# Expert stages of a two-layer trunk: which rows the indirect DMAs move, the order of splitting, and 8 KB pieces of weights

## What is computed

```python
D_MODEL, N_EXPERTS, N_GROUPS, TOPK_EXPERTS, D_EXPERT = 1024, 16, 4, 2, 512

def grouped_moe(h, w_router, b_router, w_gate, w_up, w_down):
    probs = softmax(h @ w_router + b_router)
    g_sel = argmax over the 4 groups of the sum of the group's two best probs
    vals, idx = top_k(where(in group g_sel, probs, -inf), 2)
    gates = one_hot(idx) * (vals / sum(vals)), summed over the two
    y = 0
    for e in range(N_EXPERTS):
        a = silu(h @ w_gate[e]) * (h @ w_up[e])      # (tokens, 512)
        y = y + gates[..., e:e+1] * (a @ w_down[e])  # (tokens, 1024)
    return y
```

## Time and profile before

| | |
|---|---|
| Runs | 2278.16, 2268.29, 2274.32 us; median 2274.32 |
| Profiled execution | 2277.34 us, a span of 2275.6 |
| TensorE busy | 1903.2 us of the span (84%) |
| VectorE, ScalarE, GpSimd busy | 1089.5, 768.7, 239.6 us |
| Expert stage, layer 0 | 295.0 us (958.7 to 1253.7), TensorE busy 287.0, 363 GB/s |
| Expert stage, layer 1 | 294.4 us (1923.5 to 2217.9), TensorE busy 287.1, 359 GB/s |
| Weights read in a pair | 12 units of 1.049 MB |

### The profile page before, as it was taken

How to read it: one execution, slowest core, us unless ns; L and a number is a source line. 1 busy time by engine, 2 the same in 40 slices (tenths; PEclk the granted TensorE clock), 3 DMA queues, 4 the chain that set the end, 5 groups by cost and what they waited for, 6 DMA issues and landing times.

```text
span 2275.6 us, 20410 instructions
## 1 busy us (share of the span) xinstructions
PE 1903.2 (84%) x6689; PEld 1039.8 (46%) x6689; DVE 1089.5 (48%) x1674; ACT 768.7 (34%) x993; POOL 239.6 (11%) x235
## 2 busy tenths in 40 slices
PE   2899899999899997399999479996568972999990
PEld 0443323343233334187878134343343441877870
DVE  0320352210342017298988371126742173989886
ACT  0110211111211001388786211124442021888861
POOL 0000000000000000432221120000000003122201
PEclk8899999999999997699999789995775975999995
DMA  9232172423163124699998922021002233999983
GB/s 340 102 133 77 72 277 75 158 75 111 67 247 105 54 74 147 244 359 392 392 393 332 378 77 79 20 58 38 1 1 74 85 140 102 367 393 392 393 301 122
DMA packets 194993, 412.19 MB, mean 181 GB/s; under 512 B 14382, under 2 KB 18558, under 8 KB 194877
## 3 DMA queue, kind: packets, MB, share of 16 engines
q1 hardware_dynamic: 168962, 322.26, 39.5%
q0 software_dynamic: 21248, 72.02, 8.4%
q10 hardware_dynamic: 4712, 17.02, 2.1%
HBM read 363.36 MB, written 47.90 MB: 181 GB/s over the span
## 4 chain that ended last, share of the span: by engine, by line
PE 68%; DVE 11%; DMA 8%; issue 4%; DVEq 4%; ACT 3%; POOL 1%; POOLq 0%; ACTq 0%; SPq 0%
PE bank L586 34%; PE bank L884 17%; PE bank L579 3%; DMA RING<-in_w_mod 3%; PE bank L811 3%; DMA RING<-in_w_gate 3%; ACT WH L1319 2%; PE bank L796 2%; PE bank L977 1%; PE bank L785 1%; DVEq L2228 1%; PE bank L664 1%; POOL slot_d L1644 1%; DVE WL L2083 1%; PE bank L781 1%
## 5 line engine op out<-in xcount | busy, mean ns | idle before, releaser
L586 PE MATMUL bank<-RING,HT 128*128 128x512 f32 (+3 forms) x1600 | 685.8, 584 | 15.9 <-ACT HT L1146 13.3
L2083 DVE TENSOR_TENSOR WL<-RING,WH 128x2048 fp32r<-128x2048 f32 x192 | 436.7, 2293 | 81.1 <-ACT WH L1319 79.4
L586 PEld LDWEIGHTS bank<-RING,HT 128*128 128x128 f32 (+1 forms) x1600 | 263.8, 172 | 397.8 <-issue 377.5
L1319 ACT ACTIVATE WH<-RING 128x2048 fp32r<-128x2048 f32 x192 | 364.9, 1915 | 115.4 <-PE bank L884 92.4
L579 PE MATMUL bank<-cst,M 128*128 128x128 f32 (+3 forms) x721 | 114.2, 289 | 119.4 <-DMA M<-h_d,slot_c 71.8
L884 PE MATMUL bank<-WH,HGH 128*128 128x512 f32 x512 | 204.1, 399 | 3.0 <-DVE HGL L2094 3.0
L884 PE MATMUL bank<-WL,HGH 128*128 128x512 f32 x512 | 201.3, 393 | 0.0
L884 PE MATMUL bank<-WH,HGL 128*128 128x512 f32 x512 | 201.3, 393 | 0.0
L579 PEld LDWEIGHTS bank<-cst,M 128*128 128x128 f32 (+3 forms) x721 | 92.0, 156 | 178.3 <-DMA M<-h_d,slot_c 72.8
L586 PE MATMUL bank<-RING,M 128*128 128x512 f32 (+1 forms) x320 | 138.6, 593 | 0.3 <-ACT M L1268 0.3
L884 PE MATMUL bank<-WH,ATH 128*128 128x512 f32 x256 | 102.8, 402 | 14.4 <-DVE ATL L2110 14.4
(11 more groups left out here) (277 smaller groups left out, 2095.1 us busy)
## 6 DMA issues: line engine op xcount, KB each, us to landing
RING<-in_w_gate SPq DMA_DIRECT2D x64, 1024.0 KB, 12.1
RING<-in_w_up SPq DMA_DIRECT2D x64, 1024.0 KB
RING<-in_w_down SPq DMA_DIRECT2D x64, 1024.0 KB, 12.0
RING<-in_w_mod SPq DMA_DIRECT2D x24, 2048.0 KB, 9.5
RING<-in_w_in_ret SPq DMA_DIRECT2D x12, 2048.0 KB, 12.1
RING<-in_state_ret SPq DMA_DIRECT2D x16, 1024.0 KB, 8.6
out_ret_sample<-RING POOLq DMA_DIRECT2D x16, 1024.0 KB, 6.8
RING<-in_w_in_dsa SPq DMA_DIRECT2D x5, 2048.0 KB, 14.4
```

The costliest lines, as they stand in the source:

```text
L586: last = pe.matmul(out, lhs[:, k, :], w[:, k, :], start=start and k == 0, stop=stop and k == K - 1)
L1319: act.activation(WH[:, u % SPLIT, :, :], raw(u % RAW), ACT.Copy).then_inc(S("hi_rdy"), 1)
L2083: TT(WL[:, u % SPLIT, :, :], raw(u % RAW), WH[:, u % SPLIT, :, :].bitcast(F32), ALU.subtract)\
```

## The change

The change has these parts.

1. **Only token rows move.** `h_d` has 2 x 520 rows; the store of the stage's input writes each token's row twice, at k = 0 and k = 1 (one store of 128x2x1024 for each tile). A slot holds k x 520 + token, and an empty slot holds 1040 (`none_i`), which lies beyond the end. `slot_d` is filled with 1040 near the start, and again in layer 0 after the slots have been read. The gathers have a bounds check that passes over rows beyond the end, so an empty slot moves no row.
2. **Item outputs go to their token.** `y_d` has 2 x 520 rows. Each store of `Y[j]` becomes a copy of the slots to `slot_o`, a drain and an indirect DMA with the same bounds check, in place of one plain DMA of 512 KB. At the stage's end the rows are then read by plain DMAs. The zero store to `y_d` near the start (4 MB), and ScalarE's wait for it, go away.
3. **8 KB pieces.** A partition of a weight unit holds four rows of 512 (gate, up) or two rows of 1024 (down) that lie side by side in DRAM, so it is one piece of 8 KB (SyncE's DMA is 128x2048, not 128x4x512). So partition p now holds rows 4p to 4p+3 of half a matrix, and the turned operand has to match: `turn_rows` turns every fourth column (a step of 16 bytes) and `turn_a` every second (8 bytes). A unit of down is now half of the rows and all 1024 columns, not all rows and half the columns, so both output banks of an item are written by both units.
4. **Who clears the banks.** ScalarE copies both halves of `Y[j]`; VectorE's two copies of a pair go.
5. **Order of splitting.** `take_a(1)`, the split of item 1's activations, stands ahead of unit 12 on ScalarE and VectorE, not behind it.

```diff
             def load_unit(l, e, unit, s):
...
-                src = A[w][l, e].rearrange("o (k p) n -> p (o k) n", p=P)
-                src = src[:, :, h * NB:(h + 1) * NB] if w == "w_down" else src[:, 4 * h:4 * h + 4, :]
-                sp.dma_start(raw(s), src).then_inc(S(f"raw_in{s}"), 16)
+                half = A[w].shape[2] // 2
+                src = A[w][l, e][:, h * half:(h + 1) * half, :].rearrange("o (p k) n -> p (o k) n", p=P)
+                sp.dma_start(raw(s).rearrange("p (k c) n -> p k (c n)", k=half // P), src).then_inc(S(f"raw_in{s}"), 16)
...
                     for g in range(2):
+                        part = HG[j][:, g * NB:(g + 1) * NB].rearrange("t (p q) -> t q p", q=4)
                         transposes([bank[2 * j + g][:, q * P:(q + 1) * P] for q in range(4)],
-                                   [HG[j][:, (4 * g + q) * P:(4 * g + q + 1) * P] for q in range(4)], f"hg_ps{j}")
+                                   [part[:, q, :] for q in range(4)], f"hg_ps{j}")
...
+                        part = AE.rearrange("t (h p k) -> t h k p", h=2, k=2)
                         transposes([bank[2 * j][:, q * P:(q + 1) * P] for q in range(4)],
-                                   [AE[:, q * P:(q + 1) * P] for q in range(4)], f"at_ps{j}")
+                                   [part[:, q // 2, q % 2, :] for q in range(4)], f"at_ps{j}")
...
                     def down(j, h, u):
-                        split_mm(bank[4 + 2 * j + h][:, :], ATH[:, j, :, :], ATL[:, j, :, :], u, True, True)
+                        pe.wait_ge(S("lo_rdy"), i * len(UNITS) + (UNIT0 + u + 1))
+                        for k in range(2):
+                            for n in range(2):
+                                for m, (x_, w_) in enumerate(((ATH, WH), (ATH, WL), (ATL, WH))):
+                                    done = pe.matmul(bank[4 + 2 * j + n][:, :], x_[:, j, 2 * h + k, :],
+                                                     w_[:, u % SPLIT, 2 * k + n, :], start=h == k == m == 0,
+                                                     stop=h == k == 1 and m == 2)
...
-            act.wait_ge(S("y_zero"), 16)
...
                         act.wait_ge(S(f"y_st{j}"), (i + 1) * 16)
-                        act.activation(Y[j][:, NB:D], bank[5 + 2 * j][:, :], ACT.Copy).then_inc(S(f"y_ev_a{j}"), 1)
+                        for h in range(2):
+                            act.activation(Y[j][:, h * NB:(h + 1) * NB], bank[4 + 2 * j + h][:, :], ACT.Copy)\
+                                .then_inc(S(f"y_ev{j}"), 1)
 
                     for u in range(SPLIT, SPLIT + len(UNITS)):
+                        if u == 12:
+                            take_a(1)
                         if not end or u < len(UNITS):
                             high(i, u)
...
-                        if u == 12:
-                            take_a(1)
...
-            pool.dma_start(y_items[:, NE:, :],
-                           zero_f.rearrange("p (o d) -> p o d", o=1).to_broadcast([P, ITEMS - NE, D])).then_inc(S("y_zero"), 16)
...
+                if l == 0:
+                    no_slots()
...
                     pool.indirect_dma_start(out=HG[j], out_offset=None, in_=h_d,
-                                            in_offset=bass.IndirectOffsetOnAxis(ap=slot_c[:, j:j + 1], axis=0))\
+                                            in_offset=bass.IndirectOffsetOnAxis(ap=slot_c[:, j:j + 1], axis=0),
+                                            bounds_check=2 * TOK - 1, oob_is_err=False)\
                         .then_inc(S(f"rows_in{j}"), 16)
 
                 def store(j, k):
-                    pool.wait_ge(S(f"y_ev_d{j}"), (first + k) + 2)
-                    pool.wait_ge(S(f"y_ev_a{j}"), (first + k) + 2)
-                    pool.dma_start(y_items[:, bass.ds(k * 2 + j, 1), :].rearrange("p o d -> p (o d)"), Y[j][:, :])\
+                    pool.wait_ge(S(f"y_ev{j}"), (first + k) * 2 + 4)
+                    nc.gpsimd.tensor_tensor(slot_o[:, j:j + 1], slot_i[:, bass.ds(k * 2 + j, 1)], zero_i[:, 0:1], ALU.add)
+                    pool.drain()
+                    pool.indirect_dma_start(out=y_d, out_offset=bass.IndirectOffsetOnAxis(ap=slot_o[:, j:j + 1], axis=0),
+                                            in_=Y[j][:, :], in_offset=None, bounds_check=2 * TOK - 1, oob_is_err=False)\
                         .then_inc(S(f"y_st{j}"), 16)
```

More of the change, by code:

```diff
@@ L131, in constants @@
     rot = np.stack([rc, rs], 1)
-    tok = np.zeros((P, TILES), np.int32)
-    tok[:, :] = (np.arange(TILES) * P)[None, :] + i[:, None]
+    tok = np.zeros((P, 2, TILES), np.int32)
+    tok[:, :, :] = (np.arange(2) * TOK)[None, :, None] + (np.arange(TILES) * P)[None, None, :] + i[:, None, None]
     return cst, np.ascontiguousarray(rot), tok
@@ L165, in trunk @@
         mod_d = dram("mod_d", (DEPTH, DEC + 1, 6 * D))
-        h_d = dram("h_d", (TOK, D))
+        h_d = dram("h_d", (2 * TOK, D))
         slot_d = dram("slot_d", (P * ITEMS, 1), I32)
-        y_d = dram("y_d", (P * ITEMS, D))
-        y_items = y_d.rearrange("(p i) d -> p i d", i=ITEMS)
+        y_d = dram("y_d", (2 * TOK, D))
         X = sb("X", [P, TILES, D])
@@ L184, in trunk @@
         rotc = sb("rotc", [P, 2, TILES, P])
-        tok = sb("tok", [P, TILES], I32)
+        tok = sb("tok", [P, 2, TILES], I32)
         zero_i = sb("zero_i", [P, ITEMS], I32)
+        none_i = sb("none_i", [P, ITEMS], I32)
         bf_cum = sb("bf_cum", [P, 2, P], BF16)
@@ L199, in trunk @@
         slot_c = sb("slot_c", [P, 2], I32)
-        dest_c = sb("dest_c", [P, 2, TILES], I32)
+        slot_o = sb("slot_o", [P, 2], I32)
         primer = sb("primer", [P, 2], I32)
@@ L1633, in experts @@
                     pool.wait_ge(S("hn"), TILES * m + t + 1)
-                    pool.dma_start(h_d[cols(t), :], HN[t % 2][0:rows(t), :]).then_inc(S(f"h_st{t % 2}"), 16)
+                    pool.dma_start(h_d.rearrange("(k t) d -> t k d", k=2)[cols(t)],
+                                   HN[t % 2][0:rows(t), :].rearrange("p (o d) -> p o d", o=1).to_broadcast([rows(t), 2, D]))\
+                        .then_inc(S(f"h_st{t % 2}"), 16)
                 if l == 0:
@@ L1685, in experts @@
                     pool.wait_ge(S(f"y_st{j}"), ((first + last) + 2) * 16)
-                nc.gpsimd.tensor_tensor(dest_c[:, :, :], dest_i[:, :, :],
-                                        zero_i[:, 0:2 * TILES].rearrange("p (k t) -> p k t", k=2), ALU.add)
-                pool.drain()
+                nc.gpsimd.tensor_tensor(slot_o[:, 0:1], slot_i[:, 0:1], zero_i[:, 0:1], ALU.add)
                 for t in range(TILES):
@@ L1693, in experts @@
                     for k in range(2):
-                        pool.indirect_dma_start(out=YG[t % 2][k][0:R, :], out_offset=None, in_=y_d,
-                                                in_offset=bass.IndirectOffsetOnAxis(ap=dest_c[0:R, k, t:t + 1], axis=0))\
+                        pool.dma_start(YG[t % 2][k][0:R, :], y_d[k * TOK + t * P:k * TOK + t * P + R, :])\
                             .then_inc(S(f"yg_in{t % 2}"), 16)
@@ L1786, in _ @@
             for j in range(2):
-                for name in ("a_rdy", "y_ev_d", "at_lo"):
+                for name in ("a_rdy", "at_lo"):
                     dve.engine_nop().then_inc(S(f"{name}{j}"), 1)
@@ L2129, in pair @@
                             take_a(0)
-                        if u == 12:
-                            take_a(1)
-                        if u == 13:
-                            if not end:
-                                take_rows(0, i + 1)
-                            take_y(0, 9)
-                        if u == 15:
-                            take_y(1, 11)
+                        if u == 13 and not end:
+                            take_rows(0, i + 1)
                 take_rows(0, first)
```

29 lines of the change are left out of this document (13 added, 16 removed).

## The result

The changed kernel takes 2280.51 us (median of 14 runs, 2271.51 to 2286.84), the kernel before in the same comparison 2272.33 (14 runs): a ratio of 1.0038, 95% interval 1.0023 to 1.0053. The forecast was 2260. The change makes the kernel slower by some 8 us, through the rival that the prediction called GpSimd's.

A forecast was written before the change was run, and what follows sets the result against it. TensorE was taken as the bound, the DMA engines closely second. Terms of -11.6 (order) and -2.5 (bytes) made -14.1, from 2277.34 to 2263.2 us, or 2260 on the median; range 2249 to 2290.

The forecast's parts named there:

- the rival that the prediction called GpSimd's: In the expert loops, GpSimd's four operations a pair become the bound: 2266 to 2310 us, chance 0.24.
- The bound: In the expert stages, TensorE bounds the kernel, with about 1.0 us of standing in each pair; DMA engines closely second.
- The order: In the loops, splitting item 1's activations earlier removes 14.4 us of waits and adds 2.8: net -11.6 us.
- the bytes: In the loops, moving only token rows cuts a pair to 13.65 MB and removes the DMA bound: -2.5 us.
- The new wait: TensorE waits for the low half of item 1's next rows: 0.2 us, 14 times, 2.8 us.
- What GpSimd pays: Four GpSimd operations of 8.5 us make 34.0 us a pair, below 35.8, so hidden: 0 taken.
- T: Time of one GpSimd operation in the loop; a pair takes 4T once T passes 8.95 us.
- The landing: Gather 0's DMA in the loop was taken to land in 6 us, 1.6 in time for TensorE.
- The 8 KB pieces: Weight loads in longer pieces are worth nothing of their own, and hurt only if slower than 382 GB/s.
- The stepped turn: TensorE's turns at a step: 0 taken, upper end 1.9 us a pair; as a rival 2288 us, chance 0.16.
- Ends: First gathers of the stages and layer 1's final store and reads: 0 taken for all, with -3 to +3 us.

The follow-up runs named there:

- e4: The kernel before with one edit, the split of item 1's activations ahead of weight unit 12: 2270.98 us, ratio 0.9990.
- e6: The kernel before with the token rows alone (bounds-checked gathers, indirect stores with copy and drain, no zero store): 2267.8 us, ratio 0.9986.
- e1: The changed kernel with semaphores in place of GpSimd's drains ahead of the loop's indirect DMAs: 2251.63 us, ratio to the kernel before 0.9901.
- e3: The changed kernel with 2 KB pieces, plain turns and the down product over column halves as before: 2262.85 us, ratio to the kernel before 0.9949.
- e9: e1 with the lower output banks copied by VectorE again, as before the change: 2252.5 us, ratio to the kernel before 0.9903.
- e5: The changed kernel with its 8 KB pieces kept and turns over neighbouring columns again: 2281.01 us, ratio to the kernel before 1.0042.
- e8: The changed kernel with semaphores for drains, 2 KB pieces, plain turns, and output bank copies shared by VectorE and ScalarE: 2251.2 us.
- e10: The kernel before with semaphores in place of the drains ahead of its gathers, nothing else: 2271.23 us, ratio 1.0001.

## Why the prediction was wrong, point by point

- **The bound, right.** TensorE was the bound with one wait a pair, and that wait does go in the changed kernel.
- **The order and the bytes, right together, wrong as a sum of two terms.** The prediction took -11.6 us for the order and -2.5 for the bytes. Alone, the order gives -0.6 in the loops (e4) and the token rows -2.0 (e6); with both and no drain it is -9.6 (e1). They are two bounds one behind the other, not two terms. For the whole change that would still have been a gain.
- **The new wait, right in place, too small.** 0.2 us were expected for item 1's rows; by the periods with and without it, it is 36.12 - 35.70 = 0.42 in the changed kernel and 35.97 - 35.43 = 0.54 with plain turns. TensorE's own rows name 0.2 us a time for it (1.4 us in six times in a layer of e3); what the rest of the longer period is was not taken apart. Sharing the copies again removes the wait (e9), and the period is then 35.85.
- **What GpSimd pays, the step that failed.** I took 8.5 us an operation as the mean of 9.2 and 7.8, and put it down to a busy VectorE. An operation is the landing of the DMA ahead and 0.9 us. So the store's landing had to be looked up, not the gather's issue; and the price hung on what else was in the DMA engines. The mean period of 38.15 us makes T = 9.5.
- **The landing, the second half of the same error.** "With half the bytes and DMA engines below saturation I take a landing of 6 us." It was 9.0: half the rows land no sooner (e6), and the longer pieces make it later (e3 and e5). With 8.6 for the mean and 0.9, T is 9.5 and 4T is 38.1, on the slower side of the rival's own point of 9.2. The rival had the place (the gather of item 0), the price of a T and the point from which it decides, though not the drain; I gave it 0.24. By its price T = 9.5 adds 14 x (38.1 - 36.64) - 2.5 = 18 us, and the loops grew by 18.7; the medians by 8, and the rest lies outside the loops, unexplained.
- **The 8 KB pieces, wrong.** "Worth nothing of their own": they cost 18 us through GpSimd's landings (e3, e5). Where no drain is in the way they keep the weights in time (e9 against e8).
- **The stepped turn, right that it hardly shows.** Of the range from 0 to 1.9 us a pair it is 0.27. The rule of the Trainium skill that spoke against it (Advanced Engine Details and Errata, SBUF Cachelines) is borne out in the load at a step of 16 bytes, 210 against 141 ns. At `turn_a`'s step of 8 bytes, where two words share a line, the load takes 202, and the rule's two hits do not hide that. The 8 columns from which I argued could not show either.
- **Ends.** At layer 1's end the store and the read of 2.89 and 5.31 us became 3.14 and 4.57, inside the bounds.

## What to carry to other kernels

When an engine issues DMAs one behind the other, set each start against the landing of the one ahead: a constant distance says that something waits for the landing, and then the price of one more is a landing, not an issue. A semaphore on the small copy does what the drain was there for, without the wait; a drain that is left then takes the time of the first one (e10), so all of a stage's drains have to go. And two edits that each relieve another bound are priced together, and a longer piece in one queue is priced in the landings of the others.

## What the runs showed that I had not expected

- Within a loop a GpSimd drain lasts until the DMA that GpSimd issued before it has landed: the next starts 0.76 to 0.96 us after the landing, in 34 cases of two kernels, plain stores included.
- The first GpSimd drain of a stage lasts 4 to 7 us with no packet of GpSimd's queue under way, and when the earlier drains go, the one at the stage's end lasts that long (6.00 and 6.88 us in place of 1.25, e10).
- A gather of 128 slots lands no sooner when about half of its rows are passed over: 8.4 and 7.1 us (e6) against 8.4 and 7.0. A row that is passed over leaves a packet of 4 bytes.
- 8 KB pieces of weights in place of 2 KB lengthen the landings of GpSimd's 4 KB rows from 6.9 to 8.6 us to 7.8 to 9.2, while TensorE's work and the bytes are the same.
- A load of 128 weights at a step of 16 bytes takes 210 ns against 141, at a step of 8 bytes 202, and a turn pays some 10 ns of it.
